# Prompt heads split inside the sample streams, reciprocals spread ahead of the logits, stream masks added on GpSimd, and edits at the edges of the stages

## The reference

```
layer 0:  x = x + sparse_attention(rmsnorm(x));  x = x + mlp(rmsnorm(x))
layer 1:  x = x + mamba2_ssd(rmsnorm(x));        x = x + mlp(rmsnorm(x))
y = rmsnorm(x)

sparse_attention(h):  q, k, v, qi, ki, wi = h @ w_in          # 16 heads of 64, 4 kv heads, 8 index heads
    score = einsum(relu(qi . ki), wi), -inf where not visible (chunks of 64)
    top   = the 128 (prompt) or 132 (sample) best keys of a query
    logits = q . k / 8 + rel_bias[bucket(key - query)], over the chosen keys only
    out   = softmax(logits) . v;   return out @ w_o
mlp(h):  a = relu(h @ w_up);  return (a * a) @ w_down         # 1024 -> 4096 -> 1024
```

## Time and profile before

| | |
|---|---|
| median of 3 runs | 1895.78 us (1894.93 to 1898.64) |
| the profiled execution | 1895.32 us, span 1893.4 us |
| busy in the span | PE 1848.0 us (98%), PEld 1737.0 (92%), DVE 1271.5 (67%), ACT 801.7 (42%), POOL 303.5 (16%) |
| transfers | 176.88 MB, mean 93 GB/s |

### The profile page before, as it was taken

The page is one execution under the profiler, slowest core; times in us unless marked ns, Lnnn a source line. Parts: engine busy times, 40 slices in busy tenths (PEclk is TensorE's granted clock), DMA queues, the critical chain, the costliest instruction groups (busy, mean ns, idle before and its releaser), DMA issues.

```text
span 1893.4 us, 35381 instructions
## 1 busy us (share of the span) xinstructions
PE 1848.0 (98%) x13223; PEld 1737.0 (92%) x13223; DVE 1271.5 (67%) x2357; ACT 801.7 (42%) x1435; POOL 303.5 (16%) x356
## 2 busy tenths in 40 slices
PE   8899899999999999999999999999999999999998
PEld 7777566899999999999999999999899999999998
DVE  4388875447758586447787888888554775858653
ACT  4232674334334343334465544656333434434332
POOL 0001651110000000022333343332112000000001
PEclk9999999999999999999999999999999999999999
DMA  6732203331322223322433444335423132222321
GB/s 154 128 74 53 64 24 125 77 95 57 112 62 73 84 78 94 97 55 82 129 101 123 130 133 133 102 122 164 148 67 110 51 112 62 83 75 87 92 68 56
DMA packets 311571, 176.88 MB, mean 93 GB/s; under 512 B 39888, under 2 KB 305040, under 8 KB 310416
## 3 DMA queue, kind: packets, MB, share of 16 engines
q1 hardware_dynamic: 308752, 172.49, 32.3%
q10 hardware_dynamic: 2688, 2.62, 0.5%
HBM read 155.18 MB, written 19.72 MB: 92 GB/s over the span
## 4 chain that ended last, share of the span: by engine, by line
PE 86%; DVE 4%; issue 4%; ACT 3%; DMA 1%; SPq 1%; DVEq 0%; POOL 0%; ACTq 0%
PE psum L206 29%; PE psum L1370 28%; PE psum L1398 14%; PE psum L589 1%; PE psum L2423 1%; PE psum L2436 1%; PE psum L2515 1%; PE psum L2450 1%; PE psum L565 1%; DMA W<-attn_w_in 1%; PE psum L593 1%; PE psum L554 1%; PE psum L542 1%; DVE conv_out L708 1%; PE psum L2354 1%
## 5 line engine op out<-in xcount | busy, mean ns | idle before, releaser
L206 PE MATMUL psum<-b2H,WH 128*128 128x320 f32 x912 | 218.2, 321 | 1.2 <-DVE xT L1616 0.9
L206 PE MATMUL psum<-b2H,WL 128*128 128x320 f32 x912 | 208.6, 310 | 0.0
L206 PE MATMUL psum<-b2L,WH 128*128 128x320 f32 x912 | 208.4, 310 | 0.0
L1370 PE MATMUL psum<-b2H,HT 128*128 128x320 f32 x816 | 186.2, 309 | 1.1 <-DVE xT L426 1.1
L1370 PE MATMUL psum<-b2L,HT 128*128 128x320 f32 x816 | 186.0, 309 | 0.0
L194 ACT ACTIVATE WH<-W 128x1024 fp32r<-128x1024 f32 x90 | 95.0, 1055 | 201.9 <-PE psum L206 161.5
L198 DVE TENSOR_TENSOR WL<-W,WH 128x1024 fp32r<-128x1024 f32 x90 | 139.7, 1552 | 55.8 <-ACT WH L194 54.9
L1398 PE MATMUL psum<-HH,HT 128*128 128x320 f32 x544 | 167.4, 308 | 1.5 <-DVE HL L1487 1.5
L1398 PE MATMUL psum<-HL,HT 128*128 128x320 f32 x544 | 167.8, 308 | 0.0
L206 PEld LDWEIGHTS psum<-b2H,WH 128*128 128x128 f32 x912 | 150.0, 190 | 16.0 <-issue 12.6
L206 PEld LDWEIGHTS psum<-b2L,WH 128*128 128x128 f32 x912 | 153.4, 189 | 0.0
(11 more groups left out here) (398 smaller groups left out, 4368.1 us busy)
## 6 DMA issues: line engine op xcount, KB each, us to landing
W<-ssm_w_in SPq DMA_DIRECT2D x98, 256.0 KB, 3.1
RW<-mlp_w_up SPq DMA_DIRECT2D x64, 256.0 KB, 3.0
RWx<-mlp_w_up SPq DMA_DIRECT2D x64, 256.0 KB, 3.0
RW<-mlp_w_down SPq DMA_DIRECT2D x64, 256.0 KB, 3.1
RWx<-mlp_w_down SPq DMA_DIRECT2D x64, 256.0 KB, 3.1
bc<-scratch_acs SPq DMA_DIRECT2D x8, 1280.0 KB, 7.5
W<-attn_w_in SPq DMA_DIRECT2D x32, 256.0 KB, 3.9
prev<-state_ssm SPq DMA_DIRECT2D x16, 512.0 KB, 5.3
```

Source lines behind the costliest of these rows:

```text
L206: last = pe.matmul(psum[0:m, 2 * b.slot + h, 0:TH], w[:, b.slot, k, 0:m], r[:, k, h * TH:(h + 1) * TH], start=(n == 0 and i == 0), stop=(n ...
L1370: last = pe.matmul(psum[:, i // 2 * 2 + h, 0:TH], w[:, k], x, start=(kx == 0 and c == 0), stop=(kx == 7 and c == 2))
```

## The change

- **Head.** `rep` and `cfar` go. The one-hot constant has one row less one, so that the bias of far keys is taken out of the table (the softmax does not see a constant). The products of line 2328 stand before `norm_pe_spread`. The 16 gathers of biases stand in the loop over Q blocks, two or three behind each slab.
- **Top-k.** The first round reads the scores themselves, without a copy; the last has no match-replace.
- **Prompt attention.** `spread_sums` stands before the logits, `copy_spread` and `scale_heads` come one unit later. `scale_heads` writes a new f32 buffer, `hF`; `heads_hi` and `heads_lo` of tile w stand in sample stream w. For t up to 1, the turned probabilities of two units are copied by one instruction. GpSimd copies the mask of far keys once per buffer instead of adding to it in each unit. The sample's top-k begins six units later.
- **Sample attention.** The mask is stored to DRAM, loaded per stream with a broadcast (`load_mask`) and added to `biasS` on GpSimd (`sample_bias`); line 2514 goes.
- **Edges.** The last O block writes other banks, and MLP 0 waits for a block less; the last row of MLP 0 has another bank and the DT product waits for fewer rows.
- **SSM.** The sample states are four products of 32 rows and 256 columns, in four banks; the second `silu` of a group comes later, `sample_states` on DVE earlier.
- **Tail.** The last row of MLP 1 is made in two halves with the sums between, the squares too; the last output tile is scaled by ACT and DVE and stored from ACT's queue.

```diff
+    onehot[half - 1] -= 1.0
+            self.out = 6 if c == B_O + 7 else 2 * self.slot
@@ def pe_sample_states(pe, u, p):
-        for k in range(2):
-            r = slice(64 * k, 64 * k + 64)
-            last = pe.matmul(bank(4 + k), xddt[r, p, SEQ:T], Bx[r, 4 * k:4 * k + 4].rearrange("p b n -> p (b n)"),
+        pe.wait_ge(pvc, 3 * u + p + 1)
...
+        for i in range(4):
+            r = slice(32 * i, 32 * i + 32)
+            last = pe.matmul(psum[:, 4 + i, 0:256], xddt[r, p, SEQ:T], Bx[r, 2 * i:2 * i + 2].rearrange("p b n -> p (b n)"),
@@ def rows_pe(pe, g):
-                    pe.wait_ge(out_free, last_block(layer, i // 2) + 1)
+                    pe.wait_ge(out_free, B_O + 6 if (g, i) == (0, 0) else last_block(layer, i // 2) + 1)
...
-        pe.wait_ge(sw_rx, 8)
+        pe.wait_ge(sw_rx, 6)
         multiply(pe, Block(B_DT), b2H, b2L, ready=(gx_lo, 16), order=ORD)
@@ SP, loop over Q blocks
+                if b < 6:
+                    for n in range((0, 2, 4, 7, 10, 13)[b], (2, 4, 7, 10, 13, 16)[b]):
+                        load_bias_p(DS * n) if n < 8 else load_bias_s(n - 8)
@@ SP, sample streams
+            def load_mask(b):
+                sp.wait_ge(bm, NU + max(2 * b - 2, 0))
+                sp.dma_start(MS[:, b % 2],
+                             skew(S["scores"], DS * b * KEYS_S, [[0, 8], [KEYS_S, DS], [1, KEYS_S]])
+                             ).then_inc((ss_in, bias_in)[b % 2], 16)
@@ GpSimd
+            def sample_bias(b):
+                pool.wait_ge((ss_in, bias_in)[b % 2], (16, 256)[b % 2] + 16 * (b // 2) + 16)
+                for a in range(2):
+                    if b:
+                        pool.wait_ge(ttr, NU + 2 * b + a - 1)
...
+                    pool.tensor_tensor(BMs[:, a], MS[:, b % 2], biasS[:, a], ALU.add).then_inc(bm, 1)
@@ TensorE, prompt units
                 turn(u)
                 turn(u + 1)
+                if u % 8 == 0 and u:
+                    spread_sums(u // 8 - 1)
                 if u + 4 < NU:
                     logits(u + 4)
                     logits(u + 5)
-                if u % 8 == 0 and u:
-                    spread_sums(u // 8 - 1)
@@ def sample_logits(b, a):
-                    pe.matmul(out, repst[:], maskS[:, lo:lo + n], start=True, stop=False)
-                    last = pe.matmul(out, qst[:, a], kpT[:, a, lo:lo + n], start=False, stop=True)
+                    last = pe.matmul(out, qst[:, a], kpT[:, a, lo:lo + n], start=True, stop=True)
@@ ACT, prompt units
-                if u % 8 == 1 and u > 8:
+                if u % 8 == 2 and u > 8:
                     copy_spread(u // 8 - 1)
-                if u % 8 == 4 and u > 8:
-                    heads_hi(u // 8 - 1)
@@ ACT, sample streams
+            for b in range(DB):
+                if b:
+                    sample_heads(b - 1)
+                sample_turned(b)
+                if b + 1 < DB:
+                    sample_exp(b + 1, 0)
+                if b + 2 < DB:
+                    sample_keys(b + 2)
+                heads_hi(b)
+                if b + 1 < DB:
+                    sample_exp(b + 1, 1)
@@ DVE, prompt units
-                if u % 8 == 2 and u > 8:
+                if u % 8 == 3 and u > 8:
                     scale_heads(u // 8 - 1)
-                if u % 8 == 5 and u > 8:
-                    heads_lo(u // 8 - 1)
@@ def heads_lo(w):
-                dve.wait_ge(oth, w + 1)
+                dve.wait_ge(oth, 3 * w + 1)
@@ def sample_step(b):
                     sample_max(b + 1, 0)
+                heads_lo(b)
                 sample_normalize(b)
```

More of the change, by code:

```diff
@@ L417, in build, with in_pair, turned_bank, turned_free @@
     NPV = NU // 2
+    def in_pair(u):
+        return UNITS[u][1] <= 1
+    def turned_bank(u):
+        return 4 + (u // 2 % 2 if in_pair(u) else u % 2)
+    def turned_free(u):
+        last = max(p for p in range(u // 2 * 2) if turned_bank(p) == turned_bank(u))
+        return last // 2 * 2 + 2 if in_pair(last) else last + 1
     LAST_PAIR = 3
@@ L425, in add_to_x @@
         xd = xT[:, d] if isinstance(d, int) else xT[:, bass.ds(d, 1)].rearrange("p o t -> p (o t)")
-        dve.tensor_tensor(halves(xd), out_all(b.slot), halves(xd), ALU.add).then_inc(out_free, 1)
+        dve.tensor_tensor(halves(xd), psum[:, b.out:b.out + 2, 0:TH], halves(xd), ALU.add).then_inc(out_free, 1)
     s2 = [S0]
@@ L1010, in ssm_group_act @@
         exp_w(act, g)
-        act.wait_ge(out_free, (Block(B_SSM + 5, 3 * g)).n + 1)
-        act.activation(sz[:, 1], sz[:, 1], ACT.Silu).then_inc(zs, 1)
     def pad_rows(pool, g, j):
@@ L1378, in rows_pe, with last_row_pe @@
                 final_turn_early(pe)
+                last_row_pe(pe)
+                return
+    def last_row_pe(pe):
+        n0 = op0(63)
+        pe.wait_ge(sw_rx, 14)
+        for i in (2, 3):
+            pe.wait_ge(sw_lo, n0 + i + 1)
+        for h in range(2):
+            for i in (2, 3):
+                n, b = n0 + i, ((0, 3), (4, 5))[i % 2][h]
+                for k in range(4):
+                    for c, (w, x) in enumerate(((HT[h_tile(n)], HH), (HT[h_tile(n)], HL), (LT[l_tile(n)], HH))):
+                        last = pe.matmul(psum[:, 2 + h, 0:TH], w[:, k], x[:, b, k],
+                                         start=(i == 2 and k == 0 and c == 0), stop=(i == 3 and k == 3 and c == 2))
+            last.then_inc(sw_mm, 1)
+            if h == 0:
+                final_sums(pe)
     def down_bank(g, i):
@@ L1764, in mlp_act @@
                 down_act(act, g, end)
-        next_act(act, layer, 7)
+        if layer:
+            act.wait_ge(acc_done, 38)
+            for h in range(2):
+                act.wait_ge(sw_rx, 16 + h)
+                act.activation(SQ[:, 1, h * TH:(h + 1) * TH], x_half(7, h), ACT.Square).then_inc(sq_ready, 1)
+        else:
+            next_act(act, layer, 7)
         if layer == 0:
@@ L1781, in mlp_dve @@
                 down_dve(dve, g, end)
-        add_row(dve, 32 * layer + 31, 1)
+        if layer:
+            for h in range(2):
+                dve.wait_ge(sw_mm, op0(63) + 3 + h)
+                dve.wait_ge(sw_cb, 56)
+                dve.tensor_tensor(x_half(7, h), psum[:, 2 + h, 0:TH], x_half(7, h), ALU.add).then_inc(sw_rx, 1)
+            dve.wait_ge(sw_rx, 17)
+        else:
+            add_row(dve, 31, 1)
         next_dve(dve, layer, 7)
@@ L1811, in final_pe, with final_squares @@
             pe.matmul(psum[:, 0, t:t + 1], ACC[:, t * P:(t + 1) * P], ones[:], start=(t == 0), stop=False)
+    def final_squares(pe, half):
+        pe.wait_ge(sq_ready, 40 + half)
+        for t in ((0, 1), (2, 3, 4))[half]:
+            last = pe.matmul(psum[:, 0, t:t + 1], SQ[:, 1, t * P:(t + 1) * P], ones[:], start=False, stop=(t == NT - 1))
+        return last
+    def final_pe(pe):
+        final_squares(pe, 0)
         pe.wait_ge(newton, 16 + 7)
@@ L1814, in final_pe @@
             y_turn(pe, t, ORD[6])
-        pe.wait_ge(sw_rx, 16)
-        for i in range(4):
+        pe.wait_ge(sw_rx, 17)
+        final_squares(pe, 1).then_inc(x_turn, 1)
+        for i in range(KC - 1):
             y_turn(pe, 2, ORD[i])
-        pe.wait_ge(sq_ready, 40)
-        for t in range(NT):
-            last = pe.matmul(psum[:, 0, t:t + 1], SQ[:, 1, t * P:(t + 1) * P], ones[:], start=False, stop=(t == NT - 1))
-        last.then_inc(x_turn, 1)
         for i in range(4, KC - 1):
@@ L3077, in _ @@
             dve.wait_ge(qz, 4)
-            sample_step(0)
-            with dve.Fori(1, DB - 1) as b:
+            for b in range(DB):
                 sample_step(b)
-            sample_step(DB - 1)
             sample_heads_lo(DB - 1)
```

292 lines of the change are left out of this document (145 added, 147 removed).

## The result

The changed kernel takes **1917.26 us** (median of 4 runs, 1913.0 to 1920.12); the kernel before, beside it, 1895.36. The ratio is 1.0113, with a 95% interval of 1.0092 to 1.0133: slower by about 21 us, outside the range that I gave. The profiled execution took 1917.93 us, its span is 1916.1.

The account below looks back on a forecast made before the run. TensorE, busy 98% of the span, was taken to bound the kernel. The terms summed to -2.8 us, from 1895.32 to 1892.5, or 1893.0 as a median; forecast 1889 to 1898 (chance 0.45), range 1877 to 1908.

Parts of the forecast that it names:

- the granted clock falls in the streams: Rival: idle waits lower TensorE's clock in seven sample streams, each 2.2 us, +15.4, 1908.4 us; chance 0.17.
- Stall per stream: Sample streams: TensorE waits 2.7 us at the heads' turn in six streams, 1.8 in the seventh, +18.0 us.
- The stage as a whole: From the first turn of sample keys to the output projection: forecast +12.7 us.
- Prompt: Prompt attention: waits on exponentials go, waits for the heads' scaling come; +1.7 us, range 0 to +6.6.
- Head: Start of the kernel: gathers' stall and low clock go, -7.5 us; bias table moved, +0.7; together -6.8.
- Mask: Sample streams: TensorE's mask product goes, 0.33 us in each of 16 places, -5.3 us; bounds 0.25 to 0.45.
- Sample states: SSM: four products overlap in four row groups, 0.63 us in place of 1.06, 16 times; -6.9 us.
- Edges: Both edges of MLP 0: waits for banks and rows go, 1.1 and 0.9 us; -2.0 us.
- Tail: End of the kernel: 1.0 us from sums, 0.5 from the last copy; -1.5 us, range 0 to -2.
- rivals on the row groups: SSM: only two row groups overlap, 1899.9 us, chance 0.10; or none overlap, 1910.4 us, chance 0.05.
- on the Q blocks: Rival: the gathers' stall moves to the Q blocks, late slabs, +3 to +7 us, 1896 to 1900; chance 0.08.
- the stall could be covered: Rival: in the sample streams the 18.0 us drops to at most 2, total 1875 to 1877 us; chance 0.15.

Follow-up runs that it names:

- e4_fill: Changed kernel, order and waits untouched, with unread products filling TensorE's waits: 7 before each turn of sample heads, 4 before each prompt tile's first weighing; 1899.24 us.
- e8_table_first: e3_both with the products of the table of biases ahead of the last chunk of block 0; 1865.44 us, ratio 0.9839 to the kernel before.
- e16_alternate: Kernel before with the spread's eight products alternating between the two halves of the partitions, as the change has them; 1891.49 us, ratio 0.9984.
- e6_gathers: Kernel before with the 16 gathers of biases behind the slabs of the Q blocks; 1887.69 us, ratio 0.9956.
- e13_small_mask: Kernel before without the mask's product, and three small SSM loads moved behind the fourth pair of MLP 0 slabs; 1890.49 us, ratio 0.9977.
- e7_pairs: e3_both with the sample states again as two products of 64 rows and 512 columns; 1880.38 us, ratio 0.9922 to the kernel before.
- e3_both: Changed kernel with both halves of the prompt heads' split moved earlier in the stream and the heads' scaling one unit earlier; 1876.71 us, ratio 0.9887.
- e5_high_only: Changed kernel with only the high half of the prompt heads' split moved, on ACT, before the first exponential; 1887.92 us, ratio 0.9956.
- e1_early: Changed kernel with the split's high half ahead of the first exponential on ACT, low half ahead of the first maximum on DVE; 1885.91 us.

## Why the prediction was wrong

**The waits were right, the clock was not.** The sum had every wait in its place: the heads' turn released by DVE's second maximum, the weighing by the scaling. It then priced them as time lost at full speed, their length and nothing more. That price is the step that failed: behind the waits the work itself ran at the lower clock, which the sum had at nothing. The rival "the granted clock falls in the streams" was the mechanism, and I gave it 0.17 because waits under 1 us had left the mean clock of their stretches at 0.97 and 1.00. That was also a wrong reading: the 0.97 of the prompt's attention before is no even clock, it is one fall to the lower level, and it came behind two waits under 1 us:

```profile
189.75 0.33 PE L2436 MATMUL psum<-cst,PR 128*128 128x128 f32 x1 [0.87 <-ACT PR L2697]
192.15 0.48 PE L2436 MATMUL psum<-cst,PR 128*128 128x128 f32 x1 [0.96 <-ACT PR L2697]
192.00:195.00 3.00, 2.85 (x14) 2.07 (x15) 1.34 (x7) 1.30 (x8) 1.03 (x2) 0.50 0.33 91
```

So the trace of before had falls behind a wait of 4.59 and behind short ones, and none of its rows spoke for a clock of 1.00 behind 2.7. By e4_fill the clock is 18 of the 21 us.

**The rival was also too small.** It stood only for the streams. The prompt's waits for the scaling (six of 1.9 to 2.2, one of 1.07), which the prediction had worked out too, brought the clock down as well, at four of the seven boundaries: the prompt's attention is +7.6, and 7.8 of that go with PE kept busy. In the streams the clock costs 1.3 to 2.6 each (a period of 10.9 to 12.2 against 9.64), near the 2.2 of the rival.

**Term by term.**
- *Stall per stream*, 2.7 forecast, 3.24 measured. The chain is as worked out; the low half was taken at its median, 0.70, with 1.12 as a bound. In each of six streams it took 1.2 beside GpSimd's add of the new mask, and 0.69 in the last two, which have no add beside it. That is 0.5 of the 0.54 by which the stall was off. The stage as a whole was forecast at +12.7; with the clock kept up (e4_fill) it is +16.1 (77.8 against 61.7), and the lower clock adds 10.8. In e8_table_first, where the add ends as the half begins, it takes 0.69:

```profile
279.75 0.69 DVE L3054 TENSOR_TENSOR b1L<-hF,b1H 128x512 fp32r<-128x512 f32 x1 [0.44 <-ACT b1H L2801]
278.27 1.33 POOL L2341 TENSOR_TENSOR BMs<-MS,biasS 128x528 f32<-128x528 f32 x1 [0.17 <-POOL BMs L2341]
```

- *Prompt*, +1.7 forecast: 13.2 us of waits for the scaling against 13.0 worked out, while the waits on reciprocals are 1.3 in place of the 2.7 that I let stay. With the idle time filled (e4_fill) the stage takes 100.2, as before (100.3), with the spread's alternating order in it, -3.1 (e16_alternate), which I had not counted. Without that it would be +3.0, an estimate from these two, inside the range of 0 to +6.6. The lower clock adds 7.8, which makes the measured +7.6.
- *Head*, -6.8 forecast. The gathers' part was right: -7.5 forecast, -7.6 at the first logits in e6_gathers. The other part, +0.7 for the table, was the wrong one: the wait for the last low part grew to 1.80, with a lower clock behind it, and the whole came out at -5.3, in a stage whose end differs by 4 us between traces of the same code.
- *Mask*, -5.3 forecast, -4.1 measured (e13_small_mask): 0.26 per product by the time and 0.24 by the period of a stream, at my lower bound of 0.25. It is the 0.23 of the long product alone; the 0.1 that I had added for the short one was an estimate, and nothing of it shows.
- *Sample states*, -6.9 forecast for two by two: 0.64 in place of 1.06, -0.42 each.

```profile
1055.78 0.71 PE L575 MATMUL psum<-Bx,xddt 32*128 32x256 f32 x8
1056.42 0.56 PE L203 MATMUL psum<-b2H,WH 128*128 128x320 f32 x2
```

The four row groups do overlap, in all 16 places. The rule of the Trainium skill, "TensorE: Matmul & The Clock Gate", Part 3, would have given, by an estimate, 1.3 times a single product and -5.6; 0.64 in place of 1.06 makes -6.7 over the 16 places, nearer to four at once, and e7_pairs against e3_both gives -7.2 between stages. In the changed kernel 2.6 of it come back once: the wait that the four banks need makes PE stand for a copy on ACT, and the clock is low behind it.
- *Edges*, -2.0 forecast: both waits are gone, and the second gives -1.2. The first gain is lost to a low clock behind the streams' last wait; in e8_table_first the output projection takes 57.1 against 58.4 before, the 1.1 forecast and a little more.
- *Tail*, -1.5 forecast, +0.3 measured. The stretch behind the last product is 0.9 shorter (12.9 against 13.8). The sums, 1.2 us of PE, now stand between the halves of the last row and make that product later by as much. No run has this edit by itself.

The rivals on the row groups and on the Q blocks fall with e7_pairs and e6_gathers. That the stall could be covered was right for another order (e5_high_only), not for this one.

**What stays open.** What sets when queue 8 moves its 16 KB, and so why it gets through before the loads in one run and not in another of nearly the same times. That PE stops for want of instructions is read from the order of events; no view names a releaser. `ssm_d` alone was not moved. The edits to the top-k, the copies by pairs, GpSimd's mask of far keys, the mask's way through DRAM and the `silu` were not run by themselves.

## What to carry to other kernels

Price a new wait of the matrix engine twice: its length, and the slower clock in the work behind it; here the second made 18 of 21 us, and waits of 2 us were long enough to bring it. When work is moved to another stage, write down what stands ahead of it on each engine's queue, and put it where that engine idles: the same two instructions cost 31 us in one place and nothing a few lines earlier. And try a gain again once the waits are gone, as a stage that ends earlier can run into something that was hidden, like the small loads here.

## What the hardware showed that I had not expected

- Idle times of 3.24 brought the granted clock to its lower level every time (6 of 6), 1.95 every second time (3 of 6), 1.9 to 2.2 at four of six tiles, and at five of six in e1_early, whose waits there are the same; filling the idle time with products that nobody reads kept it at 1.00 in the streams.
- A DVE subtraction of two operands in SBUF took 1.20 to 1.21 beside a GpSimd add of 128x528 (6 of 6) and 0.69 without it (2 of 2).
- Eight products with two halves of the output partitions took 1.09 at a tile alternating; in two blocks of four, their busy time was about 0.5 more (12.6 against 8.7 over eight tiles).
- Two loads of 4 KB in pieces of 4 bytes (`ssm_d`) kept one DMA engine busy for some 17 us at 106 pieces a microsecond, and in most traces the next 16 KB of instructions moved only as they ran out. In the four of them in which the 16 KB before had come 28.1 to 29.3 us earlier, PE stopped for 3.4 to 5.9 us with no releaser.
